# Six different start remainders for the split weight tiles of a two-block transformer kernel

## What is computed

```python
# first block: rmsnorm, stick-breaking attention, then dilated attention; SwiGLU after each
h = h + stick_breaking(q, k, v) @ w_o_a
h = h + (silu(hn @ w_gate) * (hn @ w_up)) @ w_down
h = h + dilated_attention(rope(q), kv_blocks) @ w_o_b
# second block: HGRN2 mixer, then windowed attention with sinks; convolved gated FFN after each
h = layer_norm(ALPHA * h + hgrn2_mixer(h, ...), ...)
h = layer_norm(ALPHA * h + conv_ffn(h, w_in, conv_w, conv_b, w_out), ...)
h = layer_norm(ALPHA * h + swa_sink_mixer(h, k, v, ...), ...)
```

## Time and profile before

| | us |
|---|---|
| median of two runs | 2457.31 |
| the two runs | 2456.37 and 2458.25 |
| profiled execution, span | 2456.5 |
| TensorE busy | 2418.6 |
| VectorE busy | 1394.3 |
| ScalarE busy | 908.5 |
| GpSimd busy | 159.8 |

### The profile page before, as it was taken

The page is one execution under the profiler, slowest core; times in us unless marked ns, Lnnn a source line. Parts: engine busy times, 40 slices in busy tenths (PEclk is TensorE's granted clock), DMA queues, the critical chain, the costliest instruction groups (busy, mean ns, idle before and its releaser), DMA issues.

```text
span 2456.5 us, 31236 instructions
## 1 busy us (share of the span) xinstructions
PE 2418.6 (98%) x11642; PEld 1974.2 (80%) x11642; DVE 1394.3 (57%) x2270; ACT 908.5 (37%) x1299; POOL 159.8 (7%) x171
## 2 busy tenths in 40 slices
PE   9999999999999999999999999999999999999998
PEld 8777888888777788888788887888888877888886
DVE  4676555433666555542366765766643665766643
ACT  4454322223666432222333332533321564433312
POOL 0000000000000000000020000000030451000031
PEclk9999999999999999999999999999999999999999
DMA  4112222223122233222311112222223312322232
GB/s 173 61 60 78 95 94 94 86 94 103 61 69 69 86 97 100 94 77 94 122 68 68 51 68 95 86 94 94 93 87 106 135 53 78 103 94 94 85 112 94
DMA packets 61078, 218.93 MB, mean 89 GB/s; under 512 B 6805, under 2 KB 7349, under 8 KB 60864
## 3 DMA queue, kind: packets, MB, share of 16 engines
q1 hardware_dynamic: 58464, 208.28, 25.5%
q0 software_dynamic: 2064, 8.97, 1.0%
q10 hardware_dynamic: 464, 0.48, 0.1%
HBM read 215.59 MB, written 2.12 MB: 89 GB/s over the span
## 4 chain that ended last, share of the span: by engine, by line
PE 88%; DVE 6%; ACT 4%; issue 1%; DMA 0%; DVEq 0%; SPq 0%; ACTq 0%
PE ps L261 25%; PE ps L263 25%; PE ps L262 25%; PE ps L2001 2%; DVE stick_left L1386 1%; PE ps L1063 1%; DVE stick_p L1392 1%; PE ps L300 1%; PE ps L301 1%; ACT window_p L1667 1%; PE ps L305 1%; PE ps L1190 1%; PE ps L1051 1%; PE ps L1210 1%; PE ps L1077 1%
## 5 line engine op out<-in xcount | busy, mean ns | idle before, releaser
L261 PE MATMUL ps<-xh,wh 128*128 128x512 f32 x1832 | 729.3, 398 | 3.9 <-DVE wl L255 2.1
L263 PE MATMUL ps<-xh,wl 128*128 128x512 f32 x1832 | 715.1, 390 | 0.0
L262 PE MATMUL ps<-xl,wh 128*128 128x512 f32 x1832 | 714.2, 390 | 0.0
L247 ACT ACTIVATE wh<-raw 128x1024 fp32r<-128x1024 f32 x331 | 347.8, 1055 | 507.4 <-PE ps L263 470.8
L255 DVE TENSOR_TENSOR wl<-raw,wh 128x1024 fp32r<-128x1024 f32 x331 | 408.1, 1234 | 200.2 <-ACT wh L247 198.4
L261 PEld LDWEIGHTS ps<-xh,wh 128*128 128x128 f32 x1832 | 344.8, 188 | 77.8 <-issue 6.5
L263 PEld LDWEIGHTS ps<-xh,wl 128*128 128x128 f32 x1832 | 344.5, 188 | 73.1
L262 PEld LDWEIGHTS ps<-xl,wh 128*128 128x128 f32 x1832 | 345.0, 188 | 70.4 <-issue 2.2
L261 PE MATMUL ps<-wh,up_ah 128*128 128x512 f32 x528 | 205.7, 390 | 1.1 <-DVE wl L428 1.1
L262 PE MATMUL ps<-wl,up_ah 128*128 128x512 f32 x528 | 205.4, 389 | 0.0
L263 PE MATMUL ps<-wh,up_al 128*128 128x512 f32 x528 | 205.4, 389 | 0.0
(11 more groups left out here) (300 smaller groups left out, 3307.8 us busy)
## 6 DMA issues: line engine op xcount, KB each, us to landing
raw<-weights SPq DMA_DIRECT2D x387, 512.0 KB, 3.5
cst<-rows_d POOLq DMA_DIRECT2D x9, 512.0 KB, 4.8
hgrn_mask<-levels POOLq DMA_DIRECT2D x1, 2048.0 KB, 7.8
window_bias<-bias_rows POOLq DMA_DIRECT2D x1, 2048.0 KB, 9.4
hT<-x_t SPq DMA_DIRECT2D x7, 256.0 KB, 6.4
out_t<-hT SPq DMA_DIRECT2D x7, 256.0 KB, 2.1
cst<-consts SPq DMA_DIRECT2D x1, 832.0 KB, 8.9
raw<-weights SPq DMA_DIRECT2D x2, 256.0 KB, 4.1
```

Source lines behind the costliest of these rows:

```text
L247: act.activation(wh[slot][:, :], raw[slot][:, :], ACT.Copy).then_inc(hi_done, 1)
L261: pe.matmul(out, w_hi, m_hi, start=first, stop=False, **kw)
L262: pe.matmul(out, w_hi, m_lo, start=False, stop=False, **kw)
L263: return pe.matmul(out, w_lo, m_hi, start=False, stop=last, **kw)
```

## The change

Each of the six split tiles is allocated 128 floats (512 bytes) longer, and `wh` and `wl` become slices of 1024 floats that begin some floats into it. `HI_AT` and `LO_AT` give the place in floats: 16, 64 and 192 bytes for the high parts of slots 0, 1 and 2, and 32, 128 and 256 bytes for the low parts. All instructions, waits and transfers, and their order on each engine, are the same as before. The tiles that follow move up by 3072 bytes in a partition and keep their remainder. In the profile the two tiles have the names `hi_room` and `lo_room`, and lines after them stand four further down (L261 becomes L265).

```diff
 SLAB = 1024
 PIECE = 256
 LINE = 512
+HI_AT = (4, 16, 48)
+LO_AT = (8, 32, 64)
...
         raw = [sb(f"raw{k}", [P, SLAB]) for k in range(SLOTS)]
-        wh = [sb(f"wh{k}", [P, SLAB], F32R) for k in range(SLOTS)]
-        wl = [sb(f"wl{k}", [P, SLAB], F32R) for k in range(SLOTS)]
+        hi_room = [sb(f"hi_room{k}", [P, SLAB + LINE // 4], F32R) for k in range(SLOTS)]
+        lo_room = [sb(f"lo_room{k}", [P, SLAB + LINE // 4], F32R) for k in range(SLOTS)]
+        wh = [hi_room[k][:, at:at + SLAB] for k, at in enumerate(HI_AT)]
+        wl = [lo_room[k][:, at:at + SLAB] for k, at in enumerate(LO_AT)]
```

## The result

The changed kernel takes 2494.89 us (median of two runs, 2494.84 and 2494.95) against 2457.31 before: 37.6 us more, a ratio of 1.0154 with an interval of 1.0137 to 1.0171. The profiled execution has a span of 2493.2 us. The forecast was 2457.3 us, no change; the kernel is slower, within the range given but not the way that was forecast.

The account below looks back on a forecast made before the run. TensorE's number of matmuls times the distance between starts was taken to bound the kernel; 2456.5 + 0 + 0 + 0 = 2456.5 us profiled, with the run median 0.8 us above: 2457.3 us, 8-in-10 range 2448 to 2575 us.

Parts of the forecast that it names:

- What bounds the kernel: Whole kernel: TensorE busy 98% of 2456.5 us; 9360 full-rate matmuls take 2112 us, 86% of the span.
- Term 1, the splits: ScalarE's copy into wh and VectorE's subtract into wl keep their times: 0 us, bounds -3 and +5 us.
- The rival with slower splits: Copy or subtract pays for its offset, slabs after a stage start come late: +5 us, 2462 us; chance 0.04.
- Term 2, the transfers: Transfers write the raw tiles, which keep their remainder, and the fetch waits for the unmoved subtract end: 0 us.
- Term 3: TensorE's reads of wh and wl at unequal remainders take no longer: 0 us, bounds -124 and +124 us.
- The slower rival: TensorE's weight load and moving stream collide more often: 0 to +124 us, at 6.7 ns +62 us, 2519 us; chance 0.34.
- the float32 rows: Attention values (L1077), stationary values 256 bytes off: 379 ns against 378 with equal remainders, offered as evidence for no cost.
- the third argument: TensorE's weight load and moving operand pass each other in every relation within 512 bytes, so offsets cost 0.
- The faster rival: Unequal remainders avoid collisions of TensorE's two reads, distance falls to 216.3 ns: -96 us, 2361 us; chance 0.12.

## Why the prediction was wrong

**What bounds the kernel** held. Full-rate matmuls, 9360 of them, set the time, 1 ns on each is 9.4 us, and what was lost came through their pace: 40.4 us by the stage table, 36.7 of them visible in the span.

**Term 1, the splits**, held: the subtract and the copy have the durations of before, 1216 and 1049 ns in the same stretch. The rival with slower splits falls with it. **Term 2, the transfers**, was taken as zero, and the stage table leaves them no visible part.

**Term 3 is the step that failed**: TensorE's reads taken at 0 where they cost 5.0 ns for each matmul in the projections. Three arguments stood for the 0. That wh costs the same as moving and as stationary operand is true but says nothing, since the distance was 0 in both roles. That float32 matmuls with values 256 bytes off cost nothing was a measurement at the one offset that is also free at full rate (the run with all weights at 256 bytes), so it showed nothing either, even apart from its half rate. And the third, that the moving stream and the load pass each other in every relation anyway, so that the start can't matter, is false: the runs with one offset a slot give the same two streams 226.7 or 233.5 ns by the start alone. It thought of the streams as independent. The distances from matmul to matmul repeat in fixed patterns of three, six or more, which looks as if each stall shifts what comes next until a pattern has settled; that reading of the patterns is argued, no run shows it.

**The slower rival** had the direction and the place right (the full-rate matmuls). It needed 5.3 ns on each for 2%; 5.0 came in the projections, and the time stayed under 2%. Its size was taken as half of the bound, 6.7 ns and +62 us, against the measured 37.6. Its bound of 13.3 ns was the right order: the most that was seen in an up stage is 6.8. Its picture, that the 13.3 ns at equal places are collisions of the load and grow, got no support from the half loads: at equal places a shorter load made the distance longer. It was given 0.34 and the forecast 0.50, on the float32 rows and the third argument. **The faster rival** falls: no offset tried goes below 226.7 ns.

The time lies within the range of 8 in 10, and within 2%, which had 0.73. Of the second, most was given to no change, so there the forecast was lucky: the effect was real and its size happened to stay below that mark.

The sentence of the prediction on the trace's limit was the one to weigh more: no row showed a full-rate matmul with unequal places, and the HGRN2 stage had a hint that I didn't use, full-rate matmuls at 229.6 ns between float32 ones, with equal places and without a wait.

The Trainium skill ("TensorE: Matmul & The Clock Gate", Part 2) says that TensorE has two independent read ports and that loading the next weights takes no read bandwidth from the running matmul. The runs don't show ports. They do show that the pace of the stream depends on where the weights lie against it, by up to 3% in an up stage, so that rule can't be used to cost a layout at nothing.

What stays open is the cause below the rule: why 256 bytes, why the cost isn't even between 0 and 256, why one offset has different paces in the token stages, and what the 13.3 ns at distance zero are. The half loads exclude one answer, a price for each piece of the load. That it is the weight load and not, say, the previous matmul's moving operand is argued and not shown, since both read the same tiles one matmul apart. That VectorE's or ScalarE's accesses to the moved tiles are in the way is unlikely: slabs of one slot repeat to 2 ns in the changed kernel, and its pace is the same with VectorE busy for 30 us in 100 as with 65. No run excludes it by itself.

## What to carry to other kernels

Put the operands of full-rate (float32r) matmuls, moving and stationary, at one remainder by 256 bytes; pieces of 512 bytes then keep it. It costs a few bytes of padding for each tile and unequal places cost up to 1.9% here. Check it by the distance between matmul starts, not by busy time, which stood at 98 and 99%. An argument from symmetry ("they meet in every relation anyway") is no price when the trace has no case with the thing changed: then give the bounds their weight, and check first whether the rows offered as nearest differ in what is asked (here 256 bytes were the same as 0).

## What the runs showed of the hardware that was not expected

- The pace of full-rate matmuls in the up stages depends on the place of the weights less that of the moving inputs, by 256 bytes: 226.7 ns at 0 and 256, 230.7 to 233.5 ns from 4 to 128 bytes, 229.2 at 192. Moving all operands together by 32 bytes changes nothing (ratio 1.0).
- It isn't a sum. One part of three moved by 32 bytes costs 6.3 ns on average for all three, nearly as much as all moved (6.4).
- With the same offsets it can take two values in turn: slabs of 5.60 and 5.44 us at 16 bytes for the high parts alone, and of 5.51 and 5.46 at 240 bytes.
- A matmul that loads 64 columns instead of 128 has a longer distance to the next one, 230.0 instead of 226.7 ns, with equal places.
